# Mixture-of-experts stage of an encoder layer: the down products in three fp32r terms, with the low weight parts made on GpSimd

## The chip, the cores and the metric

The kernel runs on one core of a Trainium2 chip. It computes one encoder layer for 512 tokens of width 1024 in a single launch. The metric is the device time of the whole launch in microseconds (us), lower is better; the time of a kernel is the median of its runs. The engines are called as in the profile: PE is TensorE, DVE is VectorE, ACT is ScalarE, POOL is GpSimd, SP is SyncE, which here only starts transfers.

## The reference, cut to what matters

The layer has a token-mixing half, which the change does not touch, and a channel-mixing half, a mixture of experts. Of the second:

```python
D_MODEL = 1024; SEQ = 512; N_EXPERTS = 64; TOP_K = 8; D_EXPERT = 256

def moe_ffn(u, router_w, router_b, exp_gate, exp_up, exp_down, ...):
    # scores, choice of 8 of 64 experts for each token, gate (T, 64) with 8 values per row
    def expert_block(args):
        ub, gb = args
        h = silu(einsum('td,edf->tef', ub, exp_gate)) * einsum('td,edf->tef', ub, exp_up)
        h = h * gb[..., None]
        return einsum('tef,efd->td', h, exp_down)
    ...
    return routed + shared
```

All of it is float32, so each expert brings 1 MB of gate weights, 1 MB of up weights and 1 MB of down weights.

## The kernel before, in words

The program is a sequence of stages; `moe` is the one that the change touches. It works in blocks: a block is one expert with up to 128 of its tokens. There are at least 64 blocks, more where an expert has over 128 tokens (68 in the profiled run). Every engine runs a program of its own, written out by hand: `first()`, then a loop whose trip holds `body(b)` for two blocks, then `last(b)`. Semaphores are what orders the engines, and the buffers `raw`, `w_hi`, `w_lo`, `wd`, `xg`, `y`, `idx` and `sidx` come in pairs, one for even and one for odd blocks.

What one block needs, in the order of the data:

- `match` (DVE, L2345): the expert's part of the routing tables is copied to `rhs` (L2348), its token positions are put relative to the block (L2349), and four operations compare them with 0 to 127 and give `S_` (L2352). PE multiplies these (`indices`, L2216), and `rows` (DVE, L2358) sums the result into `val`: which token row, which output row and which weight belongs to each place of the block. `idx` (L2363) and `sidx` (L2386) are the two row numbers as integers.
- `gather` (POOL, L2170): an indirect transfer fetches the block's token rows into `xg`. `turn_x` (PE, L2222) transposes them with 8 products into PSUM; ACT writes the high part `x_hi` in fp32r (`read_x`, L2298), DVE the rest, `x_lo` (`x_low`, L2373).
- SP loads the gate and up weights into `raw` (`load_up`, L2140). ACT makes the high parts in four pieces (`high`, L2290, the operation is L2295), DVE the low parts in four pieces (`low`, L2365, L2369). `hidden` (PE, L2232) then makes 24 products in fp32r: for each of 8 slices high by high, high by low, low by high.
- `silu` (ACT, L2304) and `product` (DVE, L2379) make the hidden values `hm`. `turn_hidden` (PE, L2252) transposes them, `read_hidden` (ACT, L2308) copies them to `hT`.
- SP loads the down weights into `wd` (`load_down`, L2144). `down` (PE, L2243, the product is L2249) multiplies `hT` by `wd` in plain float32: two products for each half of the 1024 columns. The profile counts each float32 product as two matmuls, so 8 to a block.
- `read_y` scales the first half on ACT (L2312, L2316) and the second on DVE (L2383, L2387). `scatter` (POOL, L2177, the transfer is L2180) writes the rows to memory, waits until they have landed, and only then says that `y` is free.

The blocks overlap. In `body(b)` PE does `hidden(b)`, `indices(b + 3)`, `turn_x(b + 1)`, `down(b - 1)`, `turn_hidden(b)`. ACT does `high(b + 1)`, `silu(b)`, `read_x(b + 1)`, `read_y(b - 1)`, `read_hidden(b)`. DVE does `match(b + 3)`, `low(b + 1)`, `product(b)`, `x_low(b + 1)`, `rows(b + 3)`, `read_y(b - 1)`. POOL does `gather(b + 3)` and `scatter(b - 1)`. SP starts the gate and up weights of `b + 1` when the slot is free, and the down weights of `b` when `down(b - 2)` is through.

`hold` (L28) is a wait that goes into the instruction after it; `Chain` (L34) makes DVE wait for its own earlier results.

## Time and profile before

| what | us |
|---|---|
| median of 3 runs | 1957.01 |
| lowest and highest run | 1947.66, 1977.97 |
| the profiled execution, its own time | 1955.42 |
| its span | 1953.7 |

The profile's times are from the start of the span. The expert loop runs from about 1105 to 1876 us of it; ahead of it lie the input projection, the recurrent branch and the routing, behind it the last sum and norm. A row of the timeline gives start, duration, engine, line, operation, output<-inputs, and in brackets how long the engine was idle before it and what ended that. "x4" are four instructions merged into a row, whose duration is then that of all four.

### The profile page before, as it was taken

What the parts mean: (1) busy time and instruction counts of PE and PEld (TensorE: products, weight loads), DVE (VectorE), ACT (ScalarE), POOL (GpSimd) and SP (SyncE); (2) the same over time, 40 slices, a digit from 0 to 9 for tenths busy, and PEclk for the clock granted to TensorE, in tenths of its full rate; (3) what the DMA queues carried; (4) which work ended last, traced back from release to release, by engine and by line L of the source; (5) the groups of instructions that cost most, each with busy time, mean ns of one, the idle gap of its engine ahead of it and who ended that gap; (6) DMA issues with size and microseconds to landing.
All of it is one profiled execution on the core that took longest, in us unless ns stands there. A gap on an engine that the chain in (4) does not pass through costs nothing. (4 is left out here: it accounts for less than half of the span.)

```text
span 1953.7 us, 42217 instructions
## 1 busy us (share of the span) xinstructions
PE 1723.0 (88%) x15366; PEld 1267.9 (65%) x15366; DVE 1358.9 (70%) x2513; ACT 811.6 (42%) x1327; POOL 491.2 (25%) x432
## 2 busy tenths in 40 slices
PE   3999999998688889888797699999888999999875
PEld 2787766876577778777645376666666667666532
DVE  4699996663567676765546578877766788888707
ACT  1222223441445455443300155655555566656501
POOL 2000000141644554451113013211111223332114
PEclk9899999999899999999997899999999999999988
DMA  8635853433323313222061389989888899999844
GB/s 274 193 99 173 271 171 99 130 113 98 79 44 63 66 44 72 44 61 60 3 242 54 143 314 339 371 337 345 304 304 301 314 347 345 343 351 346 326 200 199
DMA packets 259760, 389.97 MB, mean 200 GB/s; under 512 B 121923, under 2 KB 195841, under 8 KB 232240
## 3 DMA queue, kind: packets, MB, share of 16 engines
q1 hardware_dynamic: 239392, 354.28, 52.5%
q0 software_dynamic: 19872, 33.60, 4.9%
q8 instruction: 99, 1.62, 0.4%
q10 hardware_dynamic: 367, 0.22, 0.1%
q14 instruction: 30, 0.24, 0.0%
HBM read 368.33 MB, written 58.49 MB: 218 GB/s over the span
## 5 line engine op out<-in xcount | busy, mean ns | idle before, releaser
L2369 DVE TENSOR_TENSOR moe_w_lo<-moe_raw,moe_w_hi 128x1024 fp32r<-128x1024 f32 x272 | 315.1, 1220 | 42.8 <-ACT moe_w_hi L2295 42.6
L2295 ACT ACTIVATE moe_w_hi<-moe_raw 128x1024 fp32r<-128x1024 f32 x272 | 265.4, 1047 | 116.0 <-DMA moe_raw<-in_exp_up 115.6
L2249 PE MATMUL moe_pY<-moe_wd,moe_hT 128*128 128x512 f32 x544 | 248.1, 599 | 0.5 <-ACT moe_hT L2310 0.5
L2239 PE MATMUL moe_pH<-moe_w_hi,moe_x_hi 128*128 128x512 f32 x544 | 219.7, 404 | 12.0 <-issue 7.5
L2173 POOL DMA_INDIRECT moe_xg<-scratch_u2d,moe_idx x70 | 89.1, 1272 | 555.9 <-issue 240.4
L572 PE MATMUL proj_bank<-u_hi,w_hi 128*128 128x512 f32 x536 | 213.7, 399 | 8.4 <-PEq L74 6.8
L2239 PE MATMUL moe_pH<-moe_w_lo,moe_x_hi 128*128 128x512 f32 x544 | 214.3, 394 | 0.0
L2239 PE MATMUL moe_pH<-moe_w_hi,moe_x_lo 128*128 128x512 f32 x544 | 214.1, 394 | 0.0
L572 PE MATMUL proj_bank<-u_hi,w_lo 128*128 128x512 f32 x536 | 210.0, 392 | 0.0
L572 PE MATMUL proj_bank<-u_lo,w_hi 128*128 128x512 f32 x536 | 209.6, 391 | 0.0
L2249 PEld LDWEIGHTS moe_pY<-moe_wd,moe_hT 128*128 128x128 f32 x544 | 100.0, 194 | 100.3 <-issue 99.5
L798 DVE SCALAR_TENSOR_TENSOR proj_hc<-proj_hp,cwT,proj_hc 128x512 f32<-128x512 f32 x240 | 162.1, 744 | 0.0
L572 PEld LDWEIGHTS proj_bank<-u_hi,w_hi 128*128 128x128 f32 x536 | 101.3, 189 | 44.0 <-issue 22.5
L2239 PEld LDWEIGHTS moe_pH<-moe_w_hi,moe_x_hi 128*128 128x128 f32 x544 | 103.8, 191 | 34.5 <-issue 12.5
L2239 PEld LDWEIGHTS moe_pH<-moe_w_hi,moe_x_lo 128*128 128x128 f32 x544 | 103.0, 189 | 22.1
L2239 PEld LDWEIGHTS moe_pH<-moe_w_lo,moe_x_hi 128*128 128x128 f32 x544 | 103.3, 190 | 20.1
L572 PEld LDWEIGHTS proj_bank<-u_lo,w_hi 128*128 128x128 f32 x536 | 101.3, 189 | 21.5
L572 PEld LDWEIGHTS proj_bank<-u_hi,w_lo 128*128 128x128 f32 x536 | 101.4, 189 | 21.4 <-issue 1.0
L2229 PE MATMUL moe_pX<-ident,moe_xg 128*128 128x128 f32 x544 | 81.2, 295 | 33.0 <-DMA moe_xg<-scratch_u2d,moe_idx 33.0
L2376 DVE TENSOR_TENSOR moe_x_lo<-moe_pX,moe_x_hi 128x512 fp32r<-128x512 f32 x136 | 87.6, 682 | 18.8 <-ACT moe_x_hi L2301 18.7
L2180 POOL DMA_INDIRECT scratch_ybuf<-moe_y,moe_sidx x68 | 87.9, 1292 | 36.9 <-issue 24.8
L763 DVE TENSOR_TENSOR w_lo<-w,w_hi 128x1024 fp32r<-128x1024 f32 x65 | 81.5, 1255 | 17.6 <-ACT w_hi L649 17.5
(414 smaller groups left out, 3139.9 us busy)
## 6 DMA issues: line engine op xcount, KB each, us to landing
moe_raw<-in_exp_gate SPq DMA_DIRECT2D x69, 1024.0 KB
moe_raw<-in_exp_up SPq DMA_DIRECT2D x69, 1024.0 KB
moe_wd<-in_exp_down SPq DMA_DIRECT2D x68, 1024.0 KB
w<-in_w_in SPq DMA_DIRECT2D x59, 512.0 KB, 7.0
pre<-in_ada_w SPq DMA_DIRECT2D x10, 2048.0 KB, 20.5
last_yb<-scratch_ybuf SPq DMA_DIRECT2D x4, 2560.0 KB, 25.5
scratch_rkv<-proj_st SPq DMA_DIRECT2D x24, 256.0 KB, 2.0
last_yb<-scratch_ybuf SPq DMA_DIRECT2D x4, 1536.0 KB, 19.8
```

Source lines behind the costliest of these rows:

```text
L572: ins = nc.tensor.matmul(bank[b][:], a[:, slot, k], x[:, k], start=(k == 0 and m == 0), stop=(k == KC - 1 and m == 2))
L763: nc.vector.tensor_tensor(w_lo[:, n % SPLIT], w[:, n % RAW], w_hi[:, n % SPLIT].bitcast(F32), ALU.subtract) \
L798: ins = nc.vector.scalar_tensor_tensor(hc[:, k], src, cwT[:, k, j:j + 1], hc[:, k], ALU.mult, ALU.add)
L2173: pool.indirect_dma_start(out=xg[q][:], out_offset=None, in_=g["u2d"][:], in_offset=bass.IndirectOffsetOnAxis(ap=idx[q][:, 0:1], axis=0), ...
L2180: pool.indirect_dma_start(out=g["ybuf"][:], out_offset=bass.IndirectOffsetOnAxis(ap=sidx[q][:, 0:1], axis=0), in_=y[q][:], in_offset=None, ...
L2229: ins = nc.tensor.transpose(pX[h][:, k * P:(k + 1) * P], x3[:, 4 * h + k], g["ident"][:])
L2239: ins = nc.tensor.matmul(pH[:], a[:, k], w[p][:, k].rearrange("p w f -> p (w f)"), start=(k == 0 and n == 0), stop=(k == KC - 1 and n == 2))
L2249: ins = nc.tensor.matmul(pY[h][:], hT[:, f], wd[q][:, f, h * 512:(h + 1) * 512], start=(f == 0), stop=(f == 1))
L2295: nc.scalar.activation(w_hi[p][:, ks].rearrange("p k w f -> p w k f"), raw[p][:, :, ks], ACT.Copy) \
L2369: nc.vector.tensor_tensor(w_lo[p][:, ks].rearrange("p k w f -> p w k f"), raw[p][:, :, ks], w_hi[p][:, ks].rearrange("p k w f -> p w k f") ...
L2376: nc.vector.tensor_tensor(x_lo[:, 4 * h:4 * h + 4], pX[h][:].rearrange("p (k t) -> p k t", k=4), x_hi[:, 4 * h:4 * h + 4].bitcast(F32), AL ...
```

## The change

The down products go over to three fp32r terms. `wd_hi` and `wd_lo` hold the high and the low parts of one block's down weights; unlike `wd` they are single buffers. ACT writes `wd_hi` in two halves of the columns (`down_high`), each once `down` of the block before has read that half. GpSimd writes `wd_lo` (`down_low`), two subtractions of 128 x 512 to each half, from `wd` and `wd_hi`. The transposed hidden values are split too: `hT_hi` by ACT, where `hT` was, and `hT_lo` by a new DVE operation (`hidden_low`) from PSUM and `hT_hi`. `down` becomes 12 fp32r products of 512 columns where it was 4 in float32. SP waits for `wd_split`, which `down_low` raises, where it waited for `d_done`.

On GpSimd the wait for the scatter's landing becomes a function of its own (`landed`) at the end of the body. Silu is written to `hm` itself, and `hs` is gone. In `match`, `rows` and `read_y` of DVE the copy becomes an addition of a tensor of zeros, the positions and the row numbers take a second tensor where they had a scalar, and the four comparisons become one of 128 x 512.

```diff
                 e, following = expert(sp, b), expert(sp, b + 1)
                 sp.wait_ge(w_split, 4 * b)
                 load_up(b + 1, 1 - p, following)
-                sp.wait_ge(d_done, 2 * after)
+                sp.wait_ge(wd_split, 2 * after)
                 load_down(b, p, e)
...
-            def scatter(b, q, n):
+            def down_low(b, q, h):
+                hold(pool, wd_high, 2 * b + h + 1, held)
+                for f in range(2):
+                    cols = slice(h * 512, (h + 1) * 512)
+                    ins = nc.gpsimd.tensor_tensor(wd_lo[:, f, cols], wd[q][:, f, cols], wd_hi[:, f, cols].bitcast(F32), ALU.subtract)
+                ins.then_inc(wd_split, 1)
+            def scatter(b, q):
...
+            def landed(q, n):
                 hold(pool, scattered[q], 16 * (n + 1), held)
                 pool.sem_inc(y_free[q], 1)
...
             def first():
                 hold(pool, x_turned, 4, held)
                 gather(3, 1)
+                down_low(0, 0, 0)
+                down_low(0, 0, 1)
             def body(b, p, i):
                 hold(pool, x_turned, 2 * b + 4, held)
                 gather(b + 3, 1 - p)
-                scatter(b - 1, 1 - p, i + (p - 1))
+                down_low(b, p, 0)
+                scatter(b - 1, 1 - p)
+                down_low(b, p, 1)
+                landed(1 - p, i + (p - 1))
             def last(b, i):
-                scatter(b - 1, 0, i)
-                scatter(b, 1, i)
+                down_low(b, 1, 0)
+                scatter(b - 1, 0)
+                down_low(b, 1, 1)
+                landed(0, i)
+                scatter(b, 1)
+                landed(1, i)
...
             def down(b, q, n):
-                pe.wait_ge(h_read, b + 1)
-                pe.wait_ge(d_in[q], 16 * (n + 1))
+                pe.wait_ge(h_split, b + 1)
                 for h, used in ((0, y0_read), (1, y1_read)):
+                    cols = slice(h * 512, (h + 1) * 512)
                     pe.wait_ge(used, b + 1)
+                    pe.wait_ge(wd_split, 2 * b + h + 1)
                     for f in range(2):
-                        ins = nc.tensor.matmul(pY[h][:], hT[:, f], wd[q][:, f, h * 512:(h + 1) * 512], start=(f == 0), stop=(f == 1))
+                        nc.tensor.matmul(pY[h][:], hT_hi[:, f], wd_hi[:, f, cols], start=(f == 0), stop=False)
+                        nc.tensor.matmul(pY[h][:], hT_hi[:, f], wd_lo[:, f, cols], start=False, stop=False)
+                        ins = nc.tensor.matmul(pY[h][:], hT_lo[:, f], wd_hi[:, f, cols], start=False, stop=(f == 1))
                     ins.then_inc(d_done, 1)
...
-                nc.scalar.activation(hs[:], pH[:, 0:F_EXP], ACT.Silu).then_inc(silu_done, 1)
+                nc.scalar.activation(hm[:], pH[:, 0:F_EXP], ACT.Silu).then_inc(silu_done, 1)
             def read_hidden(b):
                 act.wait_ge(h_turned, b + 1)
-                nc.scalar.activation(hT[:], pT[:, 0:2 * P].rearrange("p (f t) -> p f t", f=2), ACT.Copy).then_inc(h_read, 1)
+                nc.scalar.activation(hT_hi[:], pT[:, 0:2 * P].rearrange("p (f t) -> p f t", f=2), ACT.Copy).then_inc(h_high, 1)
+            def down_high(b, q, n, used=True):
+                act.wait_ge(d_in[q], 16 * (n + 1))
+                for h in range(2):
+                    if used:
+                        act.wait_ge(d_done, 2 * b + h - 1)
+                    nc.scalar.activation(wd_hi[:, :, h * 512:(h + 1) * 512], wd[q][:, :, h * 512:(h + 1) * 512], ACT.Copy).then_inc(wd_high, 1)
             def read_y(b, q, n):
...
             def match(b, q):
...
-                ch.mark(nc.vector.tensor_copy(g["rhs"][:, q, :, FIRST_OWN:FIRST_OWN + OWN], g["own"][:, e].rearrange("p a t c -> p (a t) c")))
-                ch(nc.vector.tensor_scalar(pos[:], g["pos"][:, e].rearrange("p a t -> p (a t)"),
-                                           g["c0"][:, bass.ds(b, 1)], None, ALU.subtract))
-                for t in range(TT):
-                    ins = nc.vector.tensor_scalar(S_[:, t], g["place"][:], pos[:, t:t + 1], None, ALU.is_equal)
-                    if t < TT - 1:
-                        ch.mark(ins)
-                ch.wait()
-                ins.then_inc(s_built, 1)
+                ch.mark(nc.vector.tensor_tensor(g["rhs"][:, q, :, FIRST_OWN:FIRST_OWN + OWN], g["own"][:, e].rearrange("p a t c -> p (a t) c"),
+                                                nothing[:].unsqueeze(1).broadcast_to([P, TT, OWN]), ALU.add))
+                ch(nc.vector.tensor_tensor(pos[:], g["pos"][:, e].rearrange("p a t -> p (a t)"),
+                                           g["c0"][:, bass.ds(b, 1)].broadcast_to([P, TT]), ALU.subtract))
+                nc.vector.tensor_tensor(S_[:], g["place"][:].unsqueeze(1).broadcast_to([P, TT, P]),
+                                        pos[:].unsqueeze(2).broadcast_to([P, TT, P]), ALU.is_equal).then_inc(s_built, 1)
             def rows(b, q):
                 v.wait_ge(i_done, b + 1)
...
-                nc.vector.tensor_scalar(idx[q][:], val[:, bass.ds(b, 1), 0], float(NO_ROW), None, ALU.add).then_inc(i_ready, 1)
+                nc.vector.tensor_tensor(idx[q][:], val[:, bass.ds(b, 1), 0], no_row[:], ALU.add).then_inc(i_ready, 1)
...
-                nc.vector.tensor_tensor(hm[:], hs[:], pH[:, F_EXP:2 * F_EXP], ALU.mult).then_inc(hm_done, 1)
+                nc.vector.tensor_tensor(hm[:], hm[:], pH[:, F_EXP:2 * F_EXP], ALU.mult).then_inc(hm_done, 1)
+            def hidden_low(b):
+                v.wait_ge(h_high, b + 1)
+                nc.vector.tensor_tensor(hT_lo[:], pT[:, 0:2 * P].rearrange("p (f t) -> p f t", f=2), hT_hi[:].bitcast(F32), ALU.subtract) \
+                  .then_inc(h_split, 1)
             def read_y(b, q, n):
                 v.wait_ge(y_free[q], n + 1)
                 v.wait_ge(d_done, 2 * b + 2)
-                ch.mark(nc.vector.tensor_scalar(sidx[q][:], val[:, bass.ds(b, 1), 1], float(NO_ROW), None, ALU.add))
+                ch.mark(nc.vector.tensor_tensor(sidx[q][:], val[:, bass.ds(b, 1), 1], no_row[:], ALU.add))
```

GpSimd's loop before, from the loop's head over the two bodies of a trip (L2173 is the gather, L2180 the scatter, L30 the waits and counts of `hold`):

```order
L2131 COMPARE_AND_BRANCH
L30 ISA
L30 REGISTER_ALU
L2173 DMA moe_xg<-scratch_u2d,moe_idx 128x1024
L30 REGISTER_ALU
L2180 DMA scratch_ybuf<-moe_y,moe_sidx 4096x1024
L30 ISA x2
L30 REGISTER_ALU
L2173 DMA moe_xg<-scratch_u2d,moe_idx 128x1024
L30 REGISTER_ALU
L2180 DMA scratch_ybuf<-moe_y,moe_sidx 4096x1024
```

The same place in the changed kernel, for one body (L2175 is the gather, L2184 `down_low`, L2190 the scatter):

```order
L2133 COMPARE_AND_BRANCH
L30 ISA
L30 REGISTER_ALU
L2175 DMA moe_xg<-scratch_u2d,moe_idx 128x1024
L30 REGISTER_ALU
L2184 TENSOR_TENSOR moe_wd_lo<-moe_wd,moe_wd_hi 128x512 x2
L30 REGISTER_ALU
L2190 DMA scratch_ybuf<-moe_y,moe_sidx 4096x1024
L30 REGISTER_ALU
L2184 TENSOR_TENSOR moe_wd_lo<-moe_wd,moe_wd_hi 128x512 x2
L30 ISA x2
```

Two subtractions have come between the gather and the scatter, and two between the scatter and the wait for its landing.

DVE's program before, between two bodies of a trip (`moe_y` ends a body; the table load fetches the expert's number; `moe_S` is the comparison):

```order
L2387 TENSOR_SCALAR moe_y<-moe_pY,moe_val 128x512
L2123 ISA
L2123 TENSOR_LOAD table
L2123 ISA x2
L2348 ISA
L2348 COPY rhs<-own 128x4x4
L2349 ISA
L2349 TENSOR_SCALAR moe_pos<-pos,c 128x4
L55 ISA
L2352 TENSOR_SCALAR moe_S<-place,moe_pos 128x128 x4
L55 REGISTER_ALU
L2368 ISA
```

The same place in the changed kernel, from the new row (`moe_hT_lo`, which follows `moe_y`) to the first low part of the gate and up weights:

```order
L2416 TENSOR_TENSOR moe_hT_lo<-moe_pT,moe_hT_hi 128x256
L2125 ISA
L2125 TENSOR_LOAD table
L2125 ISA x2
L2382 ISA
L2382 TENSOR_TENSOR rhs<-own,moe_nothing 128x4x4
L2384 ISA
L2384 TENSOR_TENSOR moe_pos<-pos,c 128x4
L55 ISA
L2386 TENSOR_TENSOR moe_S<-place,moe_pos 128x512
L2399 ISA
L2400 TENSOR_TENSOR moe_w_lo<-moe_raw,moe_w_hi 128x2x2x256
```

Nothing has moved among the old DVE operations; four comparisons became one, and `hidden_low` stands between the end of `read_y` and the next `match`.

## Rows read from the trace of the kernel before

**Rows 1.** The page, engines: busy us, share of the span, instructions

```profile
PE 1723.0 (88%) x15366; PEld 1267.9 (65%) x15366; DVE 1358.9 (70%) x2513; ACT 811.6 (42%) x1327; POOL 491.2 (25%) x432
```

**Rows 2.** Stretches of the loop: length, busy per engine, clock, DMA share, GB/s

```profile
1200.00:1300.00 100.00, 97.59 (x440) 68.76 (x439) 81.00 (x162) 60.45 (x87) 25.15 (x18) 0.99 0.96 365
1700.00:1800.00 100.00, 99.53 (x440) 68.96 (x439) 81.64 (x168) 60.22 (x88) 31.45 (x20) 1.00 0.93 347
```

**Rows 3.** Timeline, `turn_hidden` of the first block, the last body's and the last block's

```profile
1132.07 0.50 PE L2255 MATMUL moe_pT<-ident,moe_hm 128*128 128x128 f32 x2
...
1850.03 0.39 PE L2255 MATMUL moe_pT<-ident,moe_hm 128*128 128x128 f32 x2
...
1868.79 0.39 PE L2255 MATMUL moe_pT<-ident,moe_hm 128*128 128x128 f32 x2
```

**Rows 4.** Timeline of one block at 1704 to 1715 us, all engines, chosen rows

```profile
1703.97 0.49 PE L2239 MATMUL moe_pH<-moe_w_hi,moe_x_hi 128*128 128x512 f32 x1
...
1705.58 0.18 DVE L2348 COPY rhs<-own 128x16 bf16 x1 [0.60 <-issue]
...
1706.01 0.74 DVE L2352 TENSOR_SCALAR moe_S<-place,moe_pos 128x128 bf16<-128x128 bf16 x4
...
1706.98 4.63 DVE L2369 TENSOR_TENSOR moe_w_lo<-moe_raw,moe_w_hi 128x1024 fp32r<-128x1024 f32 x4 [0.23 <-ACT moe_w_hi L2295]
...
1709.32 0.39 PE L2239 MATMUL moe_pH<-moe_w_hi,moe_x_lo 128*128 128x512 f32 x1
...
1710.53 1.96 POOL L2180 DMA_INDIRECT scratch_ybuf<-moe_y,moe_sidx  x1 [0.30 <-issue]
1710.64 3.60 PE L2249 MATMUL moe_pY<-moe_wd,moe_hT 128*128 128x512 f32 x8
...
1711.53 0.41 DVE L2381 TENSOR_TENSOR moe_hm<-moe_hs,moe_pH 128x256 f32<-128x256 f32 x1
...
1711.86 1.28 DVE L2376 TENSOR_TENSOR moe_x_lo<-moe_pX,moe_x_hi 128x512 fp32r<-128x512 f32 x2
...
1713.06 0.16 DVE L2362 TENSOR_REDUCE moe_val<-moe_pI 128x12 f32 x1
...
1714.08 0.39 PE L2255 MATMUL moe_pT<-ident,moe_hm 128*128 128x128 f32 x2
...
1714.40 0.15 DVE L2386 TENSOR_SCALAR moe_sidx<-moe_val 128x1 int32 x1 [1.00 <-PE moe_pY L2249]
...
1714.55 0.75 DVE L2387 TENSOR_SCALAR moe_y<-moe_pY,moe_val 128x512 f32<-128x512 f32 x1
...
1715.38 0.18 DVE L2348 COPY rhs<-own 128x16 bf16 x1
```

**Rows 5.** Timeline at 403 to 408 us, DVE beside POOL, in the projection stage

```profile
403.32 1.22 DVE L763 TENSOR_TENSOR w_lo<-w,w_hi 128x1024 fp32r<-128x1024 f32 x1
403.35 2.34 POOL L535 TENSOR_TENSOR pre<-pre,inb 128x512 f32<-128x512 f32 x1
404.45 0.74 DVE L777 SCALAR_TENSOR_TENSOR proj_st<-proj_bank,mu,proj_st 128x511 f32<-128x511 f32 x1
...
405.77 1.29 POOL L537 TENSOR_TENSOR pre<-inb,pre 128x512 f32<-128x512 f32 x1
405.89 2.25 DVE L763 TENSOR_TENSOR w_lo<-w,w_hi 128x1024 fp32r<-128x1024 f32 x1
```

**Rows 6.** Groups: a GpSimd subtraction's shape with DVE elsewhere; ACT's high parts

```profile
L1209 POOL TENSOR_TENSOR rwkv_KB<-rwkv_bb,rwkv_Ls 128x512 f32<-128x512 f32 x4 | 5.1, 1266 | 0.0
...
L2295 ACT ACTIVATE moe_w_hi<-moe_raw 128x1024 fp32r<-128x1024 f32 x272 | 265.4, 1047 | 116.0 <-DMA moe_raw<-in_exp_up 115.6
```

**Rows 7.** The line of the scatter (L2180): instructions, and issue to landing

```profile
L2180 POOL DMA_INDIRECT scratch_ybuf<-moe_y,moe_sidx x68: 980/1014/1970, 1146.2 to 1875.7; - x68
...
DMA to landing us min/median/max: 2.5/7.7/12.3
```

**Rows 8.** Timeline at 900 us: a DVE operation of two tensors, 128 x 512

```profile
900.53 1.03 DVE L1627 TENSOR_TENSOR rwkv_terms<-rwkv_A,rwkv_X 128x512 f32<-128x512 f32 x1
```

More of the change, by code:

```diff
@@ L2100, in moe @@
         pos = s.sb("pos", [P, TT])
-        hs, hm = s.sb("hs", [P, F_EXP]), s.sb("hm", [P, F_EXP])
-        hT = s.sb("hT", [P, 2, P])
+        hm = s.sb("hm", [P, F_EXP])
+        wd_hi, wd_lo = (s.sb(n, [P, 2, D], F32R) for n in ("wd_hi", "wd_lo"))
+        hT_hi, hT_lo = (s.sb(n, [P, 2, P], F32R) for n in ("hT_hi", "hT_lo"))
         y = [s.sb(f"y{p}", [P, D]) for p in range(SLOTS)]
         val = s.sb("val", [P, NBT, GRP])
+        nothing, no_row = s.sb("nothing", [P, OWN], BF16), s.sb("no_row", [P, 1])
         idx = [s.sb(f"idx{p}", [P, 1], I32) for p in range(SLOTS)]
@@ L2113, in moe @@
         (s_built, i_done, i_ready, x_zero, x_turned, x_high, x_split, w_high, w_split, h_done, silu_done, hm_done,
-         h_turned, h_read, d_done, y0_read, y1_read, dch, held, rows_in) = (s.sem(n) for n in (
+         h_turned, h_high, h_split, wd_high, wd_split, d_done, y0_read, y1_read, dch, held, rows_in) = (s.sem(n) for n in (
              "s_built i_done i_ready x_zero x_turned x_high x_split w_high w_split h_done silu_done hm_done "
-             "h_turned h_read d_done y0_read y1_read dch held rows_in").split())
+             "h_turned h_high h_split wd_high wd_split d_done y0_read y1_read dch held rows_in").split())
         block = ctx.enter_context(nc.Block())
@@ L2324, in first @@
                 read_x(1)
+                down_high(0, 0, 0, False)
                 read_hidden(0)
@@ L2331, in body @@
                 read_y(b - 1, 1 - p, i + (p - 1))
+                down_high(b, p, i)
                 read_hidden(b)
@@ L2336, in last @@
                 read_y(b - 1, 0, i)
+                down_high(b, 1, i)
                 read_hidden(b)
@@ L2385, in read_y @@
                 v.wait_ge(d_done, 2 * b + 2)
-                ch.mark(nc.vector.tensor_scalar(sidx[q][:], val[:, bass.ds(b, 1), 1], float(NO_ROW), None, ALU.add))
+                ch.mark(nc.vector.tensor_tensor(sidx[q][:], val[:, bass.ds(b, 1), 1], no_row[:], ALU.add))
                 nc.vector.tensor_scalar(y[q][:, 512:D], pY[1][:], val[:, bass.ds(b, 1), 2], None, ALU.mult).then_inc(y1_read, 1)
+            ch.mark(nc.vector.memset(nothing[:], 0.0))
+            ch(nc.vector.memset(no_row[:], float(NO_ROW)))
             for b in range(2):
@@ L2402, in first @@
                 rows(3, 1)
+                hidden_low(0)
             def body(b, p, i):
-                ch.enter(b - 1, 7)
+                ch.enter(b - 1, 4)
                 match(b + 3, 1 - p)
@@ L2411, in body @@
                 read_y(b - 1, 1 - p, i + (p - 1))
+                hidden_low(b)
                 assert ch.n - ch.start == ch.length, ch.n - ch.start
@@ L2415, in last @@
             def last(b, i):
-                ch.enter(b - 1, 7)
+                ch.enter(b - 1, 4)
                 product(b)
                 read_y(b - 1, 0, i)
+                hidden_low(b)
                 read_y(b, 1, i)
```

## The prediction

> **What bounds the kernel now.** I read the page first: PE is busy 88% of the span, DVE 70%, POOL 25% [rows 1]. An average over stages does not say what a change in one stage is worth, so I took the busy time by stretches next. In the expert loop PE is busy 98 to 100 of 100 us at the full granted clock, DVE 81 to 82, ACT 60, the transfer engines move 347 to 365 GB/s at a busy share of 0.93 to 0.96 [rows 2]. So PE bounds the loop, and the transfers stand close behind it.
>
> The period of a block is the distance between two `turn_hidden`. From block 0 to block 66 there are 66 of them in 1850.03 - 1132.07 = 717.96 us, 10.88 each; 40 of them are 10.23 to 10.25 us, and that is PE's own length. The rest, 717.96 - 66 x 10.24 = 42 us in all, are blocks in which PE waited, mostly between 1290 and 1540 us for a late gather. The last distance, with the end of the loop, is 18.76 [rows 3].
>
> I then read one block in the timeline. PE: `hidden` has 24 products from 1703.97 on, the last begins at 1709.32, so one each 5.35 / 23 = 0.233 us. `down` runs from 1710.64 to `turn_hidden` at 1714.08, 3.44 us. DVE goes from its copy to `rhs` at 1705.58 to the end of `y` at 1714.55 + 0.75 = 1715.30, 9.72 us, in which it waited 0.23 for ACT and 1.00 for PE: 8.5 of work and short gaps. The next block's copy comes 0.08 later, this one's came after 0.60 idle; half of the sum is 0.34 [rows 4]. So a DVE body without waits takes 8.5 + 0.34, and with some 0.2 for semaphores in place of those waits 9.04 us. DVE has 1.2 us to spare against PE, no more.
>
> **What the change does to PE.** Four float32 products (3.44 us) become 12 fp32r products. Their price is that of `hidden`: 12 x 0.23 = 2.76. PE's own length falls from 10.24 to 9.56 us. Over 66 blocks this would be 45 us. The two waits on `wd_split` sit ahead of each half of `down`, with `turn_hidden` and the next `hidden` queued behind them; they cost nothing as long as GpSimd's low parts are ready one block ahead, which is looked at below.
>
> **ACT.** Two more operations of 1024 elements a row, 2 x 1.05 [rows 6], in front of `read_hidden` and the next `high`. ACT is busy 6.0 of 10.24 us [rows 2], so it goes to 8.1 and stays below the period. It is not on the path as long as the weights have landed; if it were, `low` would start up to 2.1 us later and DVE with it. The wait of SP's down load moves from `d_done` to `wd_split` of the same block, which comes earlier; the load can only start sooner. I cost both at nothing, with 0 to 1 us a block as bounds.
>
> **DVE.** `hidden_low` is a subtraction of 128 x 256 from PSUM; the nearest row is `moe_hm`, of that shape, 0.41 us [rows 4]. The comparison was 0.74 for four; as one of 128 x 512 I bound it by half of a low part, 4.63 / 8 = 0.58 (about 0.64 with its start), and by the 1.03 us of another operation of that size [rows 4, 8]. The tensor is dense, so I take 0.64, a gain of 0.1. The copy, the positions and the row numbers are some tens of elements at 0.15 to 0.25 either way; nothing. Sum: 9.04 + 0.41 - 0.10 = 9.35 us, below PE's 9.56. So far all would fit under PE.
>
> **DVE beside GpSimd, the term that decides.** GpSimd now does four subtractions of 128 x 512 a block. Alone one takes 1.27 us [rows 6], so 5.1 a block. DVE's low parts are subtractions with both inputs in SBUF as well. The projection stage shows what these two do to each other: GpSimd's began 0.03 us after DVE's of 1.22 us and took 2.34 where it takes 1.29; at 405.77 GpSimd was first, and DVE's `w_lo` took 2.25 where it takes 1.22 [rows 5]. In both cases the second ends 1.08 to 1.15 us after the first: they do not overlap at all. The DVE operation of 404.45, which reads PSUM and one SBUF tensor, took its usual 0.74 beside the same GpSimd instruction.
>
> One rule of the Trainium skill bears on this, SBUF — State Buffer, section Who interferes with whom: a DVE instruction with two SBUF inputs contends with a GpSimd instruction that reads SBUF, and who comes first keeps the interface for its whole length. By that rule, the rows agree in kind, but each collision would cost DVE the full 1.27 where the rows show 2.25 - 1.22 = 1.03; two of them would make 0.5 us a block more than below.
>
> How many collide? GpSimd's order is gather, low part 0, scatter, low part 1, landing. The scatter waits for DVE's `y`, and after `y` DVE has only `hidden_low`, the table load, `match` and then the four low parts, 2.2 us later. The scatter takes 1.0 to 2.0 us [rows 4, 7]. So the two subtractions of low part 1 begin as the low parts of `w` begin, and alternate with them: two collisions of 1.03 to 1.15, 2.2 us. Low part 0 waits for ACT's `wd_hi`, which follows ACT's `y`; it falls on `product`, `x_low` and `rows`, 2 us of DVE without a second SBUF input, and its end meets the two-tensor additions for `idx` and `sidx` and perhaps one low part. Bounds 0 to 2.2; I take 0.4. DVE's body: 9.35 + 2.2 + 0.4 = 11.95 us, and PE must wait for it at `hidden`, through `x_lo`.
>
> **GpSimd's own round.** Before, a scatter landed 7.7 us after its issue in the median, 2.5 to 12.3 at the ends [rows 7], and the next gather follows it. After: gather 1.5 (mean of 1.0 and 2.0), low part 0 2.5, gap 0.3, scatter to landing 7.7 (low part 1 lies within it), together 12.0. It may be less, as the gather now lies 2.5 us ahead of the scatter and the transfers have more room in a longer period: with 5.5 to landing it is 9.8. So this round stands at the same height as DVE's body, and neither alone decides.
>
> **The ends and the disturbed blocks.** In `last`, `down(b)` waits for `wd_hi` (1.05), two low parts (5.1) and a scatter between, where it waited for `hT` alone: about 3 us more. Of the 42 us of waits, what lay above 11.95 a block is 15 us (nine blocks); a longer period swallows the rest. GpSimd's round gets longer too where landings are late, so I keep 8 of them, with 0 and 20 as bounds.
>
> **Sum.** 66 x 11.95 = 788.7, against 718.0: +70.7. With +3 and +8 it is +81.7. The profiled execution took 1955.4, which is 1.6 below the median of the runs, within their spread. 1955.4 + 81.7 = 2037 us, 4.2% slower. The interval of a period from 11.2 to 12.7 gives 1955.4 + 66 x 0.32 + 3 = 1980 to 1955.4 + 66 x 1.82 + 11 = 2087.
>
> **Rivals.**
> Faster: the two engines' subtractions hardly meet, since they slide into each other's gaps. Then PE bounds at 9.56, or the transfers. 347 GB/s x 10.3 us (9.7 blocks in 100 us) is 3.57 MB a block, at the best stretch's 365 GB/s 9.8 us [rows 2]. 66 x (9.8 - 10.88) = -71, +3 for the end: 1887 us, and 1925 if the disturbed blocks keep most of their waits. For it: GpSimd is busy a quarter of the time now. Against it: DVE's two-input work is 4.63 + 0.64 + some 0.6, 5.9 us, GpSimd's 5.1; 11.0 us cannot stand in 9.8 without overlap, and 10.1 cannot even if alternating saves 0.14 each time. Chance 0.09.
> The Trainium skill, SBUF — State Buffer, section A bandwidth-pool intuition that's wrong, gives about 358 GB/s from HBM to a core. By it the floor would be 3.57 / 358, 10.0 us, and this rival 1900 us. The trace does not agree: 365 GB/s over 100 us.
>
> No change: one collision a block, as low part 1 slips behind part of `low` or DVE's waits absorb it. 9.35 + 1.1 + 0.2 is 10.65, with some waits kept 10.85; 66 x -0.03, +3, is 1956 us. For it: the port's sum of 10.1 to 11.0 allows it. Against: the scatter's place right ahead of `low`. Chance 0.23.
>
> Slower still: GpSimd's round decides, from the point where landing takes over 7.7 us after the issue. With the 9 us seen in the disturbed stretch it is 13.3; or all four subtractions collide, 9.35 + 4 x 1.1 = 13.75. At 13.3 it is 66 x 2.42 + 3 = +163: 2118 us. Chance 0.13.
>
> The forecast has 0.55. The range: below 1955 lie the faster case and some of the unchanged, above 2115 half of the last. Under 2% from 1955.4, that is 1916 to 1995 (39 us, what a measurement can tell here), lies the unchanged case; of the forecast's own spread nearly all is above 1995. That makes faster 0.09, same 0.23, slower 0.68.
>
> **What would show it right or wrong.** In the changed profile PE falls to about 80% of a stretch of the loop, waiting at `hidden` for `x_lo` on DVE. The mean of `w_lo` in the loop rises from 1.2 to about 1.7 us, with single ones of 2.2. GpSimd's subtractions take 1.3 to 2.4, and the gather waits for the scatter's landing. The down products begin 0.23 us apart. It is wrong if `w_lo` stays at 1.2 beside GpSimd, if the low parts of `wd` fall where DVE reads PSUM, or if the period is 9.6 to 10.3.

## The result, and the profile after

The changed kernel takes 2208.2 us, the median of 4 runs (2204.51 to 2211.48). The kernel before, in the same comparison, took 1967.49. Some executions of a kernel run some per cent slower at a lower granted clock; the ratios leave these out, and so does the time of e12 below. The ratio is 1.126, with a 95% interval of 1.119 to 1.133: slower by an eighth. I had forecast slower, but by 4.2%, and my range ended at 2115. The profiled execution took 2204.51 with a span of 2202.7.

The page's engine line and two groups of it, to be read against [rows 1, 6]:

```profile
PE 1808.9 (82%) x15638; PEld 1385.9 (63%) x15638; DVE 1735.2 (79%) x2373; ACT 943.3 (43%) x1463; POOL 801.2 (36%) x704
...
L2400 DVE TENSOR_TENSOR moe_w_lo<-moe_raw,moe_w_hi 128x1024 fp32r<-128x1024 f32 x272 | 495.9, 1880 | 1.4 <-ACT moe_w_hi L2319 1.4
L2184 POOL TENSOR_TENSOR moe_wd_lo<-moe_wd,moe_wd_hi 128x512 fp32r<-128x512 f32 x272 | 345.7, 1298 | 17.4 <-ACT moe_wd_hi L2341 13.9
L2175 POOL DMA_INDIRECT moe_xg<-scratch_u2d,moe_idx x70 | 72.1, 1030 | 493.8 <-DVE moe_idx L2394 483.6
...
L2382 DVE TENSOR_TENSOR rhs<-own,moe_nothing 128x16 bf16<-128x16 bf16 x70 | 204.8, 2926 | 12.1 <-issue 12.1
```

The last row stands out. An addition of 128 x 16 elements, 0.18 us of work, has a mean of 2926 ns. `w_lo` has a mean of 1880 ns where it was 1.2 us. GpSimd's own subtractions keep their 1.3 us: only DVE pays. The same two stretches as in [rows 2] (busy time of PE, PEld, DVE, ACT, POOL, then clock, DMA share, GB/s):

```profile
1200.00:1300.00 100.00, 78.84 (x339) 60.50 (x338) 97.91 (x104) 57.95 (x77) 48.55 (x42) 0.87 0.68 259
1700.00:1800.00 100.00, 81.92 (x350) 63.07 (x350) 97.87 (x104) 57.90 (x77) 49.79 (x42) 0.86 0.64 245
```

DVE is "busy" 98 of 100 us, PE 80. The transfers, at 347 to 365 GB/s before, have fallen to 245 to 259 GB/s. One block in the timeline, DVE and GpSimd, with three of the down products:

```profile
1701.52 0.16 DVE L2394 TENSOR_TENSOR moe_idx<-moe_val,moe_no_row 128x1 int32<-128x1 f32 x1
...
1702.53 1.02 POOL L2175 DMA_INDIRECT moe_xg<-scratch_u2d,moe_idx  x1 [7.15 <-DVE moe_idx L2394]
...
1702.98 3.19 DVE L2382 TENSOR_TENSOR rhs<-own,moe_nothing 128x16 bf16<-128x16 bf16 x1
...
1703.58 2.54 POOL L2184 TENSOR_TENSOR moe_wd_lo<-moe_wd,moe_wd_hi 128x512 fp32r<-128x512 f32 x2
...
1706.07 0.15 DVE L2384 TENSOR_TENSOR moe_pos<-pos,c 128x4 f32 x1
...
1706.26 0.75 DVE L2386 TENSOR_TENSOR moe_S<-place,moe_pos 128x512 bf16<-128x512 bf16 x1
1706.28 1.01 POOL L2190 DMA_INDIRECT scratch_ybuf<-moe_y,moe_sidx  x1 [0.17 <-issue]
...
1706.93 7.42 DVE L2400 TENSOR_TENSOR moe_w_lo<-moe_raw,moe_w_hi 128x1024 fp32r<-128x1024 f32 x4
...
1707.32 2.54 POOL L2184 TENSOR_TENSOR moe_wd_lo<-moe_wd,moe_wd_hi 128x512 fp32r<-128x512 f32 x2
...
1709.69 0.48 PE L2271 MATMUL moe_pY<-moe_wd_hi,moe_hT_hi 128*128 128x512 f32 x1
...
1710.00 0.40 PE L2272 MATMUL moe_pY<-moe_wd_lo,moe_hT_hi 128*128 128x512 f32 x1
...
1710.23 0.39 PE L2273 MATMUL moe_pY<-moe_wd_hi,moe_hT_lo 128*128 128x512 f32 x1
```

Read DVE's ends against GpSimd's. `rhs` begins while the gather is being issued, stands through the rest of it and through both subtractions, and ends at 1706.17, 0.05 after the second (1706.12). The low parts of `w` begin 0.36 before the scatter ends; cut off there, the window shows the first one alone:

```profile
1706.93 4.02 DVE L2400 TENSOR_TENSOR moe_w_lo<-moe_raw,moe_w_hi 128x1024 fp32r<-128x1024 f32 x1
```

It ends at 1710.95, 1.09 after GpSimd's second subtraction (1709.86): again it waited for the whole stretch and then did its work. Both times DVE's instruction was recorded first (`rhs` 0.60 us ahead of the first subtraction, `w_lo` 0.39 ahead), and it was DVE that stood still. Four low parts take 7.42 instead of 4.62 [rows 4], 2.8 more; `rhs` takes 3.19 instead of 0.18, 3.0 more. Together 5.8 us a block in which DVE does nothing.

The period follows from the tile `moe_pT` (durations min/median/max, then first and last start), and the waits from 1300 to 2100 us show who waits for whom (us in total, times, longest):

```profile
L2279 PE MATMUL moe_pT<-ident,moe_hm x136: 270/385/493, 1135.6 to 2112.9; 128*128 128x128 f32 x136
```

```profile
POOL moe_xg L2175 <- DVE moe_idx L2394: 391.0, 55, 7.2
...
PE moe_pT L2279 <- DVE moe_hm L2412: 104.4, 55, 3.2
```

From the first to the last of these products it is 977.3 us; before it was 736.8, 0.1 more than [rows 3] give, where the last two products are one row. The 66 periods within it are 14.47 us each, nearly all alike. PE waits in every block for DVE, and GpSimd's gather waits 7.15 us for DVE's `idx`. 14.47 - 5.8 is 8.7 us: DVE's body without the collisions, below PE's 9.56.

### The profile page after: what moved, and what is told of

Read it like the earlier page. It is cut to its first block and busy times, and to the rows that moved or that the text cites. A ratio compares the mean times of both kernels' runs of the same rounds, so it can differ in the third digit from the quotient of the medians.

```text
span 2202.7 us, 43432 instructions
## 1 busy us (share of the span) xinstructions
PE 1808.9 (82%) x15638; PEld 1385.9 (63%) x15638; DVE 1735.2 (79%) x2373; ACT 943.3 (43%) x1463; POOL 801.2 (36%) x704
## 5 line engine op out<-in xcount | busy, mean ns | idle before, releaser
L2400 DVE TENSOR_TENSOR moe_w_lo<-moe_raw,moe_w_hi 128x1024 fp32r<-128x1024 f32 x272 | 495.9, 1880 | 1.4 <-ACT moe_w_hi L2319 1.4
L2184 POOL TENSOR_TENSOR moe_wd_lo<-moe_wd,moe_wd_hi 128x512 fp32r<-128x512 f32 x272 | 345.7, 1298 | 17.4 <-ACT moe_wd_hi L2341 13.9
L2260 PE MATMUL moe_pH<-moe_w_hi,moe_x_hi 128*128 128x512 f32 x544 | 266.7, 490 | 64.1 <-DVE moe_x_lo L2407 53.5
L2260 PE MATMUL moe_pH<-moe_w_lo,moe_x_hi 128*128 128x512 f32 x544 | 252.1, 463 | 0.0
L2175 POOL DMA_INDIRECT moe_xg<-scratch_u2d,moe_idx x70 | 72.1, 1030 | 493.8 <-DVE moe_idx L2394 483.6
L2260 PE MATMUL moe_pH<-moe_w_hi,moe_x_lo 128*128 128x512 f32 x544 | 250.6, 461 | 0.0
L2382 DVE TENSOR_TENSOR rhs<-own,moe_nothing 128x16 bf16<-128x16 bf16 x70 | 204.8, 2926 | 12.1 <-issue 12.1
L2260 PEld LDWEIGHTS moe_pH<-moe_w_lo,moe_x_hi 128*128 128x128 f32 x544 | 130.1, 239 | 28.4
L2279 PE MATMUL moe_pT<-ident,moe_hm 128*128 128x128 f32 x136 | 36.9, 357 | 125.8 <-DVE moe_hm L2412 125.8
L2341 ACT ACTIVATE moe_wd_hi<-moe_wd 128x1024 fp32r<-128x1024 f32 x136 | 136.9, 1050 | 1.2 <-PE moe_pY L2273 0.6
L2271 PE MATMUL moe_pY<-moe_wd_hi,moe_hT_hi 128*128 128x512 f32 x272 | 113.1, 416 | 8.0 <-POOL moe_wd_lo L2184 7.6
L2279 PEld LDWEIGHTS moe_pT<-ident,moe_hm 128*128 128x128 f32 x136 | 21.5, 206 | 153.8 <-DVE moe_hm L2412 153.7
```

Of the source, the lines that this page charges most:

```text
L2175: pool.indirect_dma_start(out=xg[q][:], out_offset=None, in_=g["u2d"][:], in_offset=bass.IndirectOffsetOnAxis(ap=idx[q][:, 0:1], axis=0), ...
L2184: ins = nc.gpsimd.tensor_tensor(wd_lo[:, f, cols], wd[q][:, f, cols], wd_hi[:, f, cols].bitcast(F32), ALU.subtract)
L2260: ins = nc.tensor.matmul(pH[:], a[:, k], w[p][:, k].rearrange("p w f -> p (w f)"), start=(k == 0 and n == 0), stop=(k == KC - 1 and n == 2))
L2271: nc.tensor.matmul(pY[h][:], hT_hi[:, f], wd_hi[:, f, cols], start=(f == 0), stop=False)
L2279: ins = nc.tensor.transpose(pT[:, f * P:(f + 1) * P], hm3[:, f], g["ident"][:])
L2341: nc.scalar.activation(wd_hi[:, :, h * 512:(h + 1) * 512], wd[q][:, :, h * 512:(h + 1) * 512], ACT.Copy).then_inc(wd_high, 1)
```

## The experiments

"Loop" below is that time from the first to the last product of `turn_hidden` in the profiled execution: 736.8 us before, 977.3 after. "Period" is the loop over its 67 distances, 11.0 before and 14.6 after; it holds the longer last distance too. A ratio is against the kernel before in the same comparison.

**1. Which part does it?** Four runs: without the subtractions, with them on DVE, the two-tensor forms alone, and the changed kernel with the old forms.

```diff
# e1_no_low: the low parts of wd are zeros
-                for f in range(2):
-                    ins = nc.gpsimd.tensor_tensor(wd_lo[:, f, cols], wd[q][:, f, cols], wd_hi[:, f, cols].bitcast(F32), ALU.subtract)
-                ins.then_inc(wd_split, 1)
+                pool.sem_inc(wd_split, 1)
# e2_low_dve: two operations of 128 x 1024 behind DVE's low
+                    nc.vector.tensor_tensor(wd_lo[:, :, cols], wd[q][:, :, cols], wd_hi[:, :, cols].bitcast(F32), ALU.subtract).then_inc(wd_split, 1)
# e3_forms_alone: the kernel before, with match, rows and read_y of the change
# e4_old_forms: the changed kernel, with match, rows and read_y of before
```

> The changed kernel without GpSimd's subtractions: wd_lo is set to zero once, and down_low keeps its waits and its count but subtracts nothing, so the low weight part is left out of the product. Everything else stays: the 12 fp32r down products, wd_hi on ACT, hidden_low and the two-tensor forms on DVE. Theory A (the second SBUF input: DVE operations with two SBUF inputs stand still while GpSimd subtracts): DVE's body falls from 14.47 us by its two long waits of about 3.0 and 2.8 us to 8.7 to 9.4, PE bounds at 9.56 and the transfers at 9.8 to 10.2; the launch takes 1885 to 1930 us, w_lo is back at a mean of 1.22 us and the copy to rhs at about 0.15. Rival B (the new chain of waits wd_hi, down_low, scatter, landing and the single buffers set the period): GpSimd's waits remain, the period falls by no more than the 5.1 us of GpSimd's work along that chain and DVE waits on semaphores: over 2000 us if only two of the subtractions lie on the chain. Rival C (the two-tensor forms are slow by themselves): rhs keeps a mean of about 2.9 us and the launch stays over 2050 us.

Measured: 2018.66 us, ratio 1.031 (1.025 to 1.036), loop 783.9, period 11.7. In part as expected: 193 of the 240 us of the loop are gone, and `w_lo` is back at 1219 ns. But it stayed 3% slower where I expected it faster. The waits from 1300 to 1900 us:

```profile
PE moe_pY L2270 <- POOLq L2182: 64.6, 36, 3.6
```

PE waits for counts that GpSimd gives behind the scatter's landing. A second bound lay under the first; part 3 tests it.

> The same low weight parts, now subtracted by DVE in two operations of 1024 elements a row, between read_y and hidden_low; GpSimd keeps only its transfers. Theory A: DVE's own body 8.7 to 9.4 plus 2 x 1.2, 11.1 to 11.8 us a block without any standing still, 66 x 3 us less than the changed kernel: 1985 to 2030 us; so the same work costs less on the busier engine. Rival B: the subtraction is still behind wd_hi and ahead of down, no gain over the changed kernel beyond the shorter operation: about 2130 us. Rival C: over 2200 us, since DVE, which is the bound, has more work and the same slow forms.

Measured: 1996.35 us, 1.020 (1.014 to 1.027), loop 764.2, within the range expected of theory A. More work on DVE, 2 x 1.2 us a block, and 213 us of the loop less than the changed kernel: what costs is not the sum of the work but that both engines do it.

> The kernel before with nothing but the two-tensor forms of rhs, pos, S, idx and sidx on DVE. Theory A: GpSimd has no subtraction here, only indirect transfers of 1 to 2 us; the forms cost what their rows say (0.15, 0.15, 0.75, 0.16, 0.16 against 0.18, 0.23, 0.74, 0.15, 0.15) and the launch is within 1% of the kernel before, 1945 to 1975 us; at most one wait of up to 1 us a block behind a gather. Rival C: rhs has a mean of about 2.9 us here too, DVE goes to 11.7 us a block, and the launch takes 2030 us or more.

Measured: 1960.22 us, 1.001 (0.994 to 1.008), as expected of theory A. The forms alone cost and bring nothing; `rhs` as an addition takes 187 ns (1150 to 1850 us):

```profile
L2349 DVE TENSOR_TENSOR rhs<-own,moe_nothing 128x16 bf16<-128x16 bf16 x65 | 12.1, 187 | 32.8 <-issue 31.4
```

> The changed kernel with the old forms of rhs, pos, S, idx and sidx (copy and scalar operations), GpSimd's subtractions kept. Theory A, if only two SBUF inputs matter: the long wait at rhs (3.0 us) shrinks to what is left when DVE comes to its first w_lo, 1.2 to 1.5 us later, so 12.5 to 13.5 us a block, 2070 to 2145 us. Theory A with the one-input forms standing still as well: no difference, 2190 to 2215 us. Rival C: 2000 us or less, since the slow forms are gone.

Measured: 2226.3 us, 1.137 (1.131 to 1.143), period 14.9. The old forms with one tensor do not escape; the nearest expectation, no difference at 2190 to 2215, is missed by 11 us:

```profile
1512.51 2.66 DVE L2382 COPY rhs<-own 128x16 bf16 x1 [0.41 <-issue]
1512.57 2.55 POOL L2184 TENSOR_TENSOR moe_wd_lo<-moe_wd,moe_wd_hi 128x512 fp32r<-128x512 f32 x2
...
1515.32 3.71 DVE L2386 TENSOR_SCALAR moe_S<-place,moe_pos 128x128 bf16<-128x128 bf16 x4
1516.33 2.48 POOL L2184 TENSOR_TENSOR moe_wd_lo<-moe_wd,moe_wd_hi 128x512 fp32r<-128x512 f32 x2
1519.01 1.22 DVE L2403 TENSOR_TENSOR moe_w_lo<-moe_raw,moe_w_hi 128x1024 fp32r<-128x1024 f32 x1
```

The copy ends 0.05 after the two subtractions, and the four comparisons (0.74 before) take 3.71 and end 0.22 after the second pair of subtractions (1518.81). Only then does `w_lo` begin, at its usual 1.22. So the collision is the same, the second time with another victim, and the two-tensor forms are not to blame.

**2. Another order on GpSimd.** If the place of the subtractions decides what they hit, moving them should help.

```diff
# e5_low_first
             def body(b, p, i):
+                down_low(b, p, 0)
+                down_low(b, p, 1)
                 hold(pool, x_turned, 2 * b + 4, held)
                 gather(b + 3, 1 - p)
-                down_low(b, p, 0)
                 scatter(b - 1, 1 - p)
-                down_low(b, p, 1)
# e7_no_low_first: e5, and zeros as in e1
# e8_split_first: e5, with half 1 of the low parts on DVE
```

> The changed kernel with GpSimd's four subtractions moved ahead of the gather in each body, nothing else. In the changed kernel the gather waits for DVE's idx, so that the subtractions come just when DVE is through with its PSUM work and goes on to rhs. Theory A (what counts is how much of DVE's work with SBUF inputs the subtractions meet): they now start when wd_hi is there, about 1.2 us before the end of w_lo, and lie beside product, x_low, rows and y; of the 5.8 us that DVE stands still about 2 to 3.5 remain, a period of 11.2 to 12.5 us, 1990 to 2075 us in all. Theory A2 (DVE stands still for every subtraction wherever it lies): no gain, 2190 to 2215 us. Rival B (GpSimd's round sets the period): the round is as long as before, 2150 us or more.

Measured: 2297.12 us, 1.179 (1.171 to 1.188), period 15.8: a miss, and the slowest of all. The collisions did fall away (`w_lo` 1256 ns in the mean), but the waits from 1300 to 1900 us now read:

```profile
POOL moe_wd_lo L2184 <- DMA scratch_ybuf<-moe_y,moe_sidx: 304.9, 38, 9.1
...
PE moe_pY L2271 <- POOL moe_wd_lo L2184: 151.8, 38, 5.0
```

The subtractions stand behind the landing of the scatter issued just before, and PE's `down` behind them. 8.5 us of landing, 5.8 of subtractions and some 1.5 of gather are 15.8, the period.

> The kernel without GpSimd's subtractions (low part set to zero once and left out of the product), now with the two counts of wd_split ahead of the gather instead of behind gather, scatter and the landing before it. In the first of these two kernels PE waited at down for that count in 36 of some 52 blocks, so the second cost of the change would be this order: low parts queue behind a landing of 8.7 us. Theory B2 (that order cost it): PE's waits at down vanish, period 9.6 to 10.9 with GpSimd's round of gather, scatter and landing as the next bound, 1910 to 1970 us against 2018.7. Rival (the transfers bound at about this rate, since they moved 312 GB/s at a share of 0.83): no gain, 2005 to 2030 us.

Measured: 2125.2 us, 1.089 (1.081 to 1.097), period 13.4. A miss again, and the same finding: with no subtraction at all, this order behind an early landing wait is 9% slower than the kernel before, where the order of e1 was 3% slower.

> The low weight parts shared out: the first half of the columns stays with GpSimd (two subtractions, ahead of the gather), the second half is one DVE subtraction of 1024 elements a row between read_y and hidden_low. Theory A: DVE 8.7 + 1.2 + what two subtractions of GpSimd cost it, 0 to 2.5; 10.2 to 12.0 us a block, 1930 to 2040 us; at the lower end it equals the kernel before. If each GpSimd subtraction costs DVE its whole length wherever it lies, 12.4 us a block, about 2070 us.

Measured: 2224.8 us, 1.143 (1.135 to 1.151). A miss for the same cause: GpSimd's subtractions waited 291 us for the scatter's landing between 1300 and 1800 us (33 times), and PE 116 us for the subtractions.

**3. Landing waited for one body later.** Then nothing on GpSimd stands behind a transfer just issued. The same edit goes to the kernel before (a first scatter of which every row number is `NO_ROW`, so that it writes nothing, makes the counts even).

```diff
# e9_before_late_wait (on before), e10_low_first_late_wait (on e5), e11_late_wait (on the changed kernel)
             def body(b, p, i):
...
+                landed(p, i)
                 scatter(b - 1, 1 - p)
-                landed(1 - p, i + (p - 1))
```

> The kernel before, with the wait for a scatter's landing moved from behind that scatter to the next body, between its gather and its scatter (a first empty scatter on the odd slot makes the count start at one). Nothing of the change is in it. Theory B2 (GpSimd's round of gather, scatter and landing, 1.5 + 0.3 + 7.7 us, makes the late gathers of the kernel before): the 42 us above 66 x 10.24 mostly vanish, 1915 to 1940 us. Rival (the transfers themselves are late there): within 0.5% of the kernel before, 1950 to 1970 us.

Measured: 1959.19 us, 1.002 (0.997 to 1.006), loop 729.1. Nothing gained, as the rival had it, so GpSimd's round did not make the 42 us of waits in the kernel before. PE's waits for gathered rows are gone (27 us in 13 waits before, none now, from 1135 to 1850 us), but ACT now waits 123 us for the up weights where it waited 64 (1300 to 1800 us): the delay has only moved to another transfer.

> The changed kernel with both orders mended on GpSimd: the four subtractions ahead of the gather, and the wait for a scatter's landing moved into the next body, ahead of the next scatter (an empty scatter on the odd slot makes the count start at one). All work is there. With the subtractions first alone DVE no longer stood still at w_lo (4.62 us for four), but the next subtractions waited for the landing, 8.5 us after the issue, and the period was 16. Theory A+B (the loss is DVE standing still in the one order, the landing in the other): both go, DVE 8.7 + 0.6, PE 9.56, GpSimd 5.1 to 5.8 + 2.6, and the transfers, 3.6 MB a block at some 340 GB/s, bound at 10.6: 1920 to 1985 us. If a GpSimd subtraction costs DVE its length wherever it lies: over 2100 us.

Measured: 1983.29 us, 1.019 (1.009 to 1.028), loop 751.9, period 11.2, with all the work of the changed kernel: a hit in time, at the upper end of the range, but not in what bounds. I had expected the transfers to bind at 10.6 us and DVE to stand still for 0.6. By the order of GpSimd's queue alone 225 of the 240 us of the loop are back. What stays (one window, then the page's groups):

```profile
1150.00:1850.00 700.00, 636.84 (x3173) 501.92 (x3172) 689.91 (x958) 517.30 (x701) 548.92 (x382) 1.00 0.89 330
```

```profile
L2406 DVE TENSOR_TENSOR moe_w_lo<-moe_raw,moe_w_hi 128x1024 fp32r<-128x1024 f32 x272 | 343.8, 1322 | 1.6 <-ACT moe_w_hi L2325 1.6
...
L2392 DVE TENSOR_TENSOR moe_S<-place,moe_pos 128x512 bf16<-128x512 bf16 x70 | 109.3, 1561 | 2.4
...
L2388 DVE TENSOR_TENSOR rhs<-own,moe_nothing 128x16 bf16<-128x16 bf16 x70 | 42.7, 610 | 9.7 <-issue 9.4
```

DVE is busy 98.6% and is the bound, at 10.7 to 11.3 us a block. The subtractions now begin near the end of `x_lo`, while DVE reads PSUM. For the 5.1 us or more that they last, DVE stands still for about 2.3 us (11.0 a block less the 8.7 of its body). `S` takes 1561 ns instead of 750, `rhs` 610, `w_lo` 1322; `y` and `hT_lo`, which read PSUM and lie beside the subtractions, keep their 0.74 and 0.41.

> The changed kernel with only the landing wait moved into the next body, the subtractions left where the change has them. Theory A (in the changed kernel itself only DVE's standing still bounds; its scatters land in 3.3 us, within the second pair of subtractions): no difference, 2190 to 2215 us, DVE at 98%. Theory B (the landing is part of what bounds the changed kernel): 2120 us or less.

Measured: 2211.1 us, 1.136 (1.125 to 1.147), loop 978.0. As expected of theory A, late waiting alone changes nothing: the landing did not bound the changed kernel, the collisions did. Both are needed together, the order (e5 has it alone) and the late wait.

**4. The transfers.** The loads of `wd` in the loop are cut to 64 of 1024 columns.

```diff
# e12_e10_no_down_loads, e13_before_no_down_loads, e16_e14_no_down_loads
-                load_down(b, p, e)
+                sp.dma_start(wd[p][:, :, 0:64], exp_down[0, e].rearrange("a (p c) d -> p (a c) d", p=P)[:, :, 0:64]).then_inc(d_in[p], 16)
# e14_e10_no_low: e10, and zeros as in e1
```

> The kernel with subtractions first and late landing wait, but from the third block on SP loads only 64 of the 1024 columns of the down weights, so the down products use stale weights; transfers fall from 3.6 to 2.6 MB a block. If transfers bound the full version: PE bounds now, 9.6 us a block, 1880 to 1900 us. If something else bounds it (GpSimd's subtractions, DVE): no more than 1% below the full version.

Measured: 1982.53 and 1987.29 us against e10's 1981.23 to 1984.88, period 11.2 in both, at 240 GB/s instead of 330. No gain: transfers do not bound e10.

> The kernel before with only 64 of 1024 columns of the down weights loaded from the third block on, so the down products use stale weights. If the transfers made the blocks above 10.24 us in the kernel before: all blocks at 10.24, 1957 - 42 = 1915 us, 1905 to 1925. If they were made by the order of waits: 1945 to 1965 us.

Measured: 1924.34 us, 0.989 (0.979 to 0.998), loop 698.0, every block from the second on 10.24; 1915 had been expected, with 1925 as the upper bound. The kernel before moved 336 GB/s from 1150 to 1850 us, this one 249:

```profile
1150.00:1850.00 700.00, 682.78 (x3023) 475.00 (x3022) 546.71 (x1104) 418.27 (x587) 205.99 (x132) 0.99 0.68 249
```

The waits of before are gone once 0.94 of the 3.6 MB a block are not moved. The load on the transfers made them, and the late gather was where it showed.

> Subtractions first and late landing wait, but the subtractions left out (low weight part zero, so it is left out of the product). If the order of GpSimd's queue was all that held the kernels without subtractions back: PE 9.56, transfers 10.4 to 10.7, 1930 to 1955 us, w_lo at 1.22. If ACT's added work, hidden_low or the single buffers hold it: over 1965 us with waits of PE on ACT or DVE in nearly every block.

Measured: 1920.12 us, 0.970 (0.960 to 0.981), loop 694.6, period 10.4, 10 us below the expected range. Against e10 it is 57 us of loop for the subtractions, and against e1 89 us for the order: the second layer of experiment e1 is mended. It is a test and no faster kernel, as it leaves the low weight part out of the product.

```profile
1150.00:1800.00 650.00, 623.27 (x3189) 506.39 (x3188) 548.92 (x955) 513.53 (x700) 134.15 (x126) 1.00 0.92 356
```

> The same with only 64 of 1024 columns of the down weights loaded from the third block on (stale weights in the down products). If transfers bound e14: PE bounds now, 9.5 to 9.6 us a block, 1870 to 1895 us, which would be the gain that fp32r alone offers. If not: as e14.

Measured: 1912.79 us, 0.969 (0.959 to 0.979), loop 674.9, period 10.1, blocks of 9.55 and 10.25 in turn. That misses the 1870 to 1895 expected if transfers bound e14. The loop is 20 us shorter than e14's, but that compares e14's slowest execution (1931.07) with the fastest here (1909.69); the medians differ by 7 us and the executions of the two overlap, so what the transfers cost e14 is not shown. For every other block being longer the trace offers a cause: between 1150 and 1800 us PE waits 31 times for DVE's `x_lo`, up to 0.5 us, and DVE's `hidden_low` waits 35 times for ACT's `hT_hi` (21.5 us in all), which stands behind the 2.0 us of `wd_hi` on ACT. No run takes this wait away.

**5. Is there a version that beats the kernel before?**

```diff
# e15_split_late_wait: e10, with half 1 of the low parts on DVE (as in e8)
# e17_low_dve_late_wait: e2, with the late wait
```

> All work done; first half of the columns subtracted by GpSimd ahead of the gather, second half by DVE, landing wait late. DVE 8.7 + 1.2 + 0.5 to 1.5 of standing still: 10.4 to 11.4 us a block, 1940 to 1990 us. If a GpSimd subtraction costs DVE its whole length here too: 12.4, 2060 us.

Measured: 1959.5 us, 0.997 (0.993 to 1.001), period 10.9, as expected.

> All subtractions on DVE, landing wait late; GpSimd has transfers only. DVE's body is 10.82 as in the kernel with the early wait (36 of its blocks were at 10.8, others at 12 to 15 behind a late gather). If the late gathers came from GpSimd's round: all at 10.8 to 10.9, 1955 to 1975 us. If from the transfers: 1985 to 2000 us, no gain.

Measured: 1969.14 us, 1.004 (1.000 to 1.008), period 11.0, as expected. Against e2 it shows that the late gathers there came from GpSimd's round. With all the work done, none was faster than the kernel before by a margin that the interval holds; e15 equals it.

## Why the prediction was wrong in size

**Right.** PE stopped being the bound, and DVE's collisions with GpSimd became it. PE is busy 80%, down products begin 0.23 us apart (1710.00, 1710.23), ACT with its two more operations (58 of 100 us) delays nothing here, and the forms cost nothing (e3). With DVE's stops gone ACT's `wd_hi` seems to get onto the path (e16).

**The step that failed** is the one that placed low part 0: "it falls on `product`, `x_low` and `rows`, 2 us of DVE without a second SBUF input ... I take 0.4." I let low part 0 wait for ACT's `wd_hi`. In fact it stands behind the gather, and the gather waits for DVE's `idx`, in `rows`. Low part 0 can only begin when DVE has left `rows`, so it meets `match`. It cost 3.0 us at `rhs`, above even my upper bound of 2.2. The period was forecast 2.5 us too short, and this term alone was 2.6 too small; the two that follow, 0.6 too small and 0.65 too large, nearly cancel.

**The price of one stretch** was mis-sized too: 2.2 for low part 1, measured 2.8. I let the engines alternate, two collisions of 1.03 to 1.15. They do not: DVE waits for both subtractions back to back, and for the end of the indirect transfer's issue ahead of them. The Trainium skill, SBUF — State Buffer, section Who interferes with whom, has the one who comes first keep the interface for its whole length; the trace shows DVE held longer than one instruction, for 3.0 us, though its `rhs` began ahead of the first subtraction.

**DVE's body** was 8.7 where I had 9.35; the 0.34 and 0.2 I had added for its start and for semaphores did not come up. So 9.35 + 2.6 = 11.95 should have been 8.7 + 5.8 = 14.5. Over 66 blocks that is 66 x 14.47 = 955.0 against 718.0: +237. The start of the loop came 3.6 us later (1135.63 for 1132.07), which I had not foreseen, and the last distance was 22.46 for 18.76, 3.7 more where I had 3. Of the 249 us between the two profiled executions 5 lie behind the loop. My 8 us for disturbed blocks were 0: all periods but the first and one short one are 14.44 to 14.50 us.

**GpSimd's own round** of 12.0 did not decide: without its wait of 7.15 us for DVE's `idx` it is 7.3. The scatter lands 3.3 us after its issue, not 7.7 (min/median/max):

```profile
DMA to landing us min/median/max: 2.5/3.3/4.0
```

It did decide where the collisions were removed (e1, e5, e7), at 8.5 to 10.3 us to landing. The rival nearest to the result was "all four subtractions collide", 13.75 us, which I had put together with another at a chance of 0.13.

**The 42 us of before** I had blamed on late gathers. e9 takes that cause away and gains nothing. e13 takes bytes away, and every block from the second on is at 10.24. With [rows 2] the transfers already stood at 0.93 to 0.96; I read the instruction that was waiting and not what held it.

## What to carry to other kernels

Where VectorE and GpSimd both work in SBUF, write their operations there on one common time line, as if on one engine, and count a whole run of GpSimd's as one piece that VectorE may have to sit out: here 5.1 us of subtractions cost VectorE 5.8, and still 2.3 in the better order (e10). What a GpSimd instruction is queued behind decides which operation of VectorE it meets; a subtraction queued behind a gather that waits for VectorE meets VectorE by construction. Put the waits for landings as late as the buffers allow, ahead of any reordering: the order that was best with late waits (e10, 1.02) was the worst with early ones (e5, 1.18).

## What the runs showed of the hardware that was not expected

- A VectorE operation of 0.18 us stood still for 3.0 us, from within a gather's issue to the end of the second subtraction behind it. In e10, where GpSimd runs four subtractions in a row, VectorE gets in between them: in one block `idx` took 0.44, `rhs` 1.28 and `S` 1.68 where they take 0.16, 0.18 and 0.75. Why it is let in there and not here is open.
- Operations with one tensor stood still as well: a copy of 128 x 16 in bf16 for 2.66 us, comparisons with a scalar in bf16 for 3 of 3.71 (e4).
- A gather with no subtraction behind it did not hold `rhs`, which began inside it (e14):

```profile
1512.97 1.02 POOL L2175 DMA_INDIRECT moe_xg<-scratch_u2d,moe_idx  x1 [2.16 <-issue]
...
1513.32 0.18 DVE L2387 TENSOR_TENSOR rhs<-own,moe_nothing 128x16 bf16<-128x16 bf16 x1 [0.87 <-issue]
```

  So it is not the transfer as such. How a subtraction that has not begun can hold an addition back that has, no run shows.
- The time from a scatter's issue to its landing did not go with the mean rate of the transfers. At 232 to 253 GB/s (1150 to 1850 us) it was 3.3 us in the changed kernel and 8.5 to 8.6 in e5 and e8. The traces differ in what SP has under way. In the changed kernel the gate and up weights were started 6 us before the scatter (at 1706.28) and land 4.8 and 7.0 us after their issue in the median; the down weights start when it has landed:

```profile
1700.04 0.34 SPq L2143 DMA_DIRECT2D moe_raw<-in_exp_gate  x1
1700.48 0.38 SPq L2144 DMA_DIRECT2D moe_raw<-in_exp_up  x1
...
1710.02 0.33 SPq L2147 DMA_DIRECT2D moe_wd<-in_exp_down  x1
```

  In e7 three loads of 1 MB start from 2.3 us before the scatter to 0.4 behind it, and its scatters take 10.3 us to land, at 273 GB/s:

```profile
1508.23 0.33 SPq L2147 DMA_DIRECT2D moe_wd<-in_exp_down  x1
...
1510.50 0.34 SPq L2143 DMA_DIRECT2D moe_raw<-in_exp_gate  x1
1510.50 1.01 POOL L2187 DMA_INDIRECT scratch_ybuf<-moe_y,moe_sidx  x1 [0.30 <-issue]
1510.94 0.38 SPq L2144 DMA_DIRECT2D moe_raw<-in_exp_up  x1
```

  This is read from the traces; no run moved the loads alone.
- PE's granted clock was 0.86 to 0.87 in the changed loop: behind each wait some products stand 0.43 us apart, the lower of its two levels (1.2 GHz), before they come 0.23 apart again. DVE is the bound there: even so PE waits 1.9 us a block in the mean for DVE's `hm`, so the clock cost nothing. In e10, whose waits at `hidden` are under 1 us, the clock was 1.00.
